# Norms in quarters over two engines, block order in a stage's first slot, and a bank-wise last slot: a two-block transformer on one core

## What is computed

```python
for l in range(2):                                   # first block
    h = rms_norm(x, norm_mix[l])
    x = x + (swa_sb_mixer if l == 0 else hgrn2_mixer)(h, ...)
    x = x + memory_cross_attention(rms_norm(x, norm_cross[l]), rms_norm(mem, norm_mem[l]), ...)
    x = x + conv_ffn(rms_norm(x, norm_ffn[l]), ...)   # up 1024 -> 2 x 2816, conv of 3, silu gate, down
x = layer_norm(ALPHA * x + pool_mixer(x), ...)        # second block; means over 2, 4, 8, 16 tokens
x = layer_norm(ALPHA * x + swiglu(x, ...), ...)
x = layer_norm(ALPHA * x + nsa_mixer(x, ...), ...)
x = layer_norm(ALPHA * x + moe_ffn(x, ...), ...)      # 8 experts, top 2, 2 x 3584 wide
```

## Time and profile before

| | |
|---|---|
| median of 3 runs | 2549.62 us (2549.35 to 2552.17) |
| the profiled execution | 2545.54 us, of it the span of the core 2543.6 us |
| TensorE matmul busy | 2435.7 us, 96% of the span |
| VectorE busy | 1924.6 us, 76% |
| ScalarE busy | 1310.6 us, 52% |
| mean granted TensorE clock | 0.988 of full speed |

### The profile page before, as it was taken

How to read it: one execution, slowest core, us unless ns; L and a number is a source line. 1 busy time by engine, 2 the same in 40 slices (tenths; PEclk the granted TensorE clock), 3 DMA queues, 4 the chain that set the end, 5 groups by cost and what they waited for, 6 DMA issues and landing times.

```text
span 2543.6 us, 43969 instructions
## 1 busy us (share of the span) xinstructions
PE 2435.7 (96%) x18390; PEld 2319.4 (91%) x18390; DVE 1924.6 (76%) x2365; ACT 1310.6 (52%) x1436; POOL 2.4 (0%) x8
## 2 busy tenths in 40 slices
PE   7899999999999999799998889999999999999998
PEld 6689999999999999799897789999999999999996
DVE  6656596888675868754656678888888888888887
ACT  3445333344443333133225357766676767676764
POOL 0000000000000000000000000000000000000000
PEclk9999999999999999999999999999999999999999
DMA  5224245532343455354331159998999999899895
GB/s 215 77 102 148 106 183 179 188 133 100 125 149 116 166 183 183 127 183 180 135 117 59 67 200 364 342 339 333 343 342 340 342 339 343 340 342 341 343 339 211
DMA packets 77283, 557.27 MB, mean 219 GB/s; under 512 B 8609, under 2 KB 8737, under 8 KB 10145
## 3 DMA queue, kind: packets, MB, share of 16 engines
q1 hardware_dynamic: 75888, 547.45, 57.9%
q10 hardware_dynamic: 1008, 6.49, 0.7%
q0 software_dynamic: 192, 0.52, 0.1%
HBM read 552.86 MB, written 1.05 MB: 218 GB/s over the span
## 4 chain that ended last, share of the span: by engine, by line
PE 69%; DVE 4%; ACT 2%; issue 1%; DMA 1%; DVEq 0%; ACTq 0%; SPq 0%
PE ps L1380 12%; PE ps L1382 12%; PE ps L1381 12%; PE ps L837 8%; PE ps L839 8%; PE ps L838 8%; PE ps L929 2%; PE ps L1420 1%; PE ps L900 1%; PE ps L1374 1%; ACT whi L496 1%; DMA raw<-stream 1%; PE ps L1177 1%; PE ps L844 0%; DVE x L1613 0%
## 5 line engine op out<-in xcount | busy, mean ns | idle before, releaser
L1506 DVE TENSOR_TENSOR wlo<-raw,whi 128x2048 fp32r<-128x2048 f32 x519 | 1186.1, 2290 | 318.1 <-ACT whi L496 259.4
L496 ACT ACTIVATE whi<-raw 128x2048 fp32r<-128x2048 f32 x519 | 993.6, 1915 | 580.1 <-PE ps L839 424.6
L837 PE MATMUL ps<-hh,whi 128*128 128x256 f32 x2080 | 599.1, 288 | 26.5 <-DVE hl L1574 21.2
L838 PE MATMUL ps<-hl,whi 128*128 128x256 f32 x2080 | 593.0, 285 | 0.0
L839 PE MATMUL ps<-hh,wlo 128*128 128x256 f32 x2080 | 592.9, 285 | 0.0
L1380 PE MATMUL ps<-whi,hh 128*128 128x256 f32 x1792 | 523.4, 292 | 3.6 <-DVE work L2193 3.6
L1382 PE MATMUL ps<-wlo,hh 128*128 128x256 f32 x1792 | 507.7, 283 | 0.0
L1381 PE MATMUL ps<-whi,hl 128*128 128x256 f32 x1792 | 507.4, 283 | 0.0
L837 PEld LDWEIGHTS ps<-hh,whi 128*128 128x128 f32 x2080 | 403.9, 194 | 31.3 <-DVE hl L1574 24.7
L838 PEld LDWEIGHTS ps<-hl,whi 128*128 128x128 f32 x2080 | 404.1, 194 | 0.3
L839 PEld LDWEIGHTS ps<-hh,wlo 128*128 128x128 f32 x2080 | 403.7, 194 | 0.0
(11 more groups left out here) (329 smaller groups left out, 2782.0 us busy)
## 6 DMA issues: line engine op xcount, KB each, us to landing
raw<-stream SPq DMA_DIRECT2D x519, 1024.0 KB, 4.9
work<-w_in ACTq DMA_DIRECT2D x1, 2240.0 KB, 8.5
stage<-stage_consts ACTq DMA_DIRECT2D x4, 512.0 KB, 4.7
work<-mem_in ACTq DMA_DIRECT2D x2, 1024.0 KB, 4.8
x<-x_in SPq DMA_DIRECT2D x1, 1024.0 KB, 4.8
out<-x SPq DMA_DIRECT2D x4, 256.0 KB, 2.3
const<-consts SPq DMA_DIRECT2D x1, 548.5 KB, 5.9
work<-work POOLq DMA_DIRECT2D x4, 128.0 KB, 2.3
```

The source lines that it names most:

```text
L496: nc.scalar.activation(whi[hi_at(g, odd)][:, :], raw[g % RAWS][:, :], ACT.Copy).then_inc(hi_ready, 1)
L837: mm(out_ap, hi_w, hi_x, start=start, stop=False, **kw)
L838: mm(out_ap, hi_w, lo_x, start=False, stop=False, **kw)
L1506: V.tensor_tensor(wlo[g % RAWS][:, :], raw[g % RAWS][:, :], whi[hi_at(g, odd)][:, :].bitcast(F32), ALU.subtract).then_inc(lo_ready[g % RAW ...
```

## The change

- RMS norms (`rms_norm`, `rms_act`): VectorE scales a quarter; ScalarE rounds it into hh; VectorE makes hl of the quarter before.
- Layer norms (`layer_norm`, `layer_norm_act`): VectorE centres, scales and makes hl; ScalarE squares, shifts (Identity with a bias) and rounds. In the last two norms nothing is rounded.
- The squares of x ahead of the norm of hg_in move from VectorE to ScalarE.
- First slots with waits: both output rows of an input block are done before the next block.
- The last down slot of the three dense layers (`down_last`) goes output by output; each finished bank releases its add on VectorE (`acc_ready`, three times, and `slot_used`); the closing zero matmuls are gone.
- Pool mixer: the first doubling reads x itself, ScalarE fills in its first column; the division by the full window is part of the subtraction, and only the first 16 columns get their own factor (`shorter`); rounding and alpha go to ScalarE.
- Dummy matmuls ahead of first slots: ab_in 14 to 10, ffn0, ffn1 and hg_in 22 to 18, ffn2 and nsa_in 32 to 22; within layer norms 24, 14, 20, 20 to 12 each; ten after ffn0 are gone.

```diff
--- before.py
+++ after.py
...
@@ -361,6 +367,14 @@
...
+        HI_AT = {0: 0, 2: 1, 3: 2, 4: 3, 6: 4, 7: 5, "pool": 6, "ln0": 7, "ln1": 8}
+
+        POOL_PAD = 16
+
+        def pool_sums(i):
+
+            return Wc(4352 * i, NB * (POOL_PAD + BLK)).rearrange("p (b t) -> p b t", b=NB)
...
@@ -512,6 +526,34 @@
...
+            def round_quarter(c, src):
+
+                nc.scalar.activation(hh[:, c * 512:(c + 1) * 512], src[:, c * 512:(c + 1) * 512], ACT.Copy).then_inc(hi_done, 1)
+
+            def rms_act(n):
+
+                norm_act(n, D, 1e-6)
+                for c in range(QUARTERS):
+                    act.wait_ge(norm_scaled, QUARTERS * HI_AT[n] + c + 1)
+                    round_quarter(c, hf)
+
+            def layer_norm_act(i):
+
+                last = i >= 2
+                for c in range(QUARTERS):
+                    act.wait_ge(ln_centred, QUARTERS * i + c + 1)
+                    nc.scalar.activation(hf[:, c * 512:(c + 1) * 512], x[:, c * 512:(c + 1) * 512], ACT.Square).then_inc(squares_ready, 1)
+                norm_act(8 + i, D, 1e-5)
+                for c in range(QUARTERS + 1):
+                    if c < QUARTERS:
+                        act.wait_ge(norm_scaled, QUARTERS * (6 + i) + c + 1)
+                        for b in (2 * c, 2 * c + 1):
+                            ins = nc.scalar.activation(xb(b), xb(b), ACT.Identity, bias=R("ln_b", 8 * i + b))
+                        ins.then_inc(x_ready, 1)
+                    if c and not last:
+                        act.wait_ge(x_ready, QUARTERS * i + c)
+                        round_quarter(c - 1, x)
...
@@ -665,11 +707,14 @@
...
-            norm_act(4, D, 1e-6)
+            for c in range(QUARTERS):
+                act.wait_ge(acc_drained, c + 1)
+                nc.scalar.activation(hf[:, c * 512:(c + 1) * 512], x[:, c * 512:(c + 1) * 512], ACT.Square).then_inc(squares_ready, 1)
+            rms_act(4)
...
@@ -733,15 +778,23 @@
...
+            for g in range(QUARTERS):
+                act.wait_ge(acc_drained, QUARTERS + g + 1)
+                nc.scalar.activation(pool_sums(1)[:, 2 * g:2 * g + 2, POOL_PAD:POOL_PAD + 1], xb(2 * g, 2).rearrange("p (b t) -> p b t", b=2)[:, :, 0:1],
+                                     ACT.Copy).then_inc(pool_first, 1)
+            for g in range(QUARTERS):
+                act.wait_ge(pool_mixed, g + 1)
+                round_quarter(g, hf)
+                nc.scalar.activation(x[:, g * 512:(g + 1) * 512], x[:, g * 512:(g + 1) * 512], ACT.Copy, scale=ALPHA).then_inc(pool_scaled, 1)
...
-            norm_act(8, D, 1e-5)
+            layer_norm_act(0)
...
@@ -854,13 +907,15 @@
...
-                for b in range(2):
-                    for c in range(NB):
-                        if h is not None and s == first and b == 0 and c % 2 == 0:
-                            pe.wait_ge(h_ready, QUARTERS * (h - 1) + c // 2 + 1)
-                        w = slice((b * NB + c) * P, (b * NB + c + 1) * P)
-                        x_hi, x_lo = (t[:, c * BLK:(c + 1) * BLK] for t in (hh, hl)) if src is None else src(c)
-                        last = split_mm(ps[:, bank, b * BLK:(b + 1) * BLK], hi[:, w], lo[:, w], x_hi, x_lo, c == 0, c == NB - 1)
+                waits = h is not None and s == first
+                by_rows = [(b, c) for b in range(2) for c in range(NB)]
+                for b, c in sorted(by_rows, key=lambda bc: bc[1]) if waits else by_rows:
+                    if waits and b == 0 and c % 2 == 0:
+                        pe.wait_ge(h_ready, QUARTERS * (h - 1) + c // 2 + 1)
+                    w = slice((b * NB + c) * P, (b * NB + c + 1) * P)
+                    x_hi, x_lo = (t[:, c * BLK:(c + 1) * BLK] for t in (hh, hl)) if src is None else src(c)
+                    last = split_mm(ps[:, bank, b * BLK:(b + 1) * BLK], hi[:, w], lo[:, w], x_hi, x_lo,
+                                    c == 0 and not (waits and b), c == NB - 1, skip_group_check=waits)
...
@@ -884,6 +939,21 @@
...
+            def down_last(ph, s, a0):
+
+                g = ph.g + s
+                hi, lo = whi[hi_at(g)], wlo[g % RAWS]
+                wait_lo(pe, g)
+                pe.wait_ge(act_ready, a0 + 2 * s + 2)
+                for b in range(NB):
+                    for c in range(2):
+                        m = slice((2 * s + c) * BLK, (2 * s + c + 1) * BLK)
+                        w = slice((c * NB + b) * P, (c * NB + b + 1) * P)
+                        last = split_mm(ps[:, 3 + b // 2, (b % 2) * BLK:(b % 2 + 1) * BLK], hi[:, w], lo[:, w], ahi[:, m], alo[:, m],
+                                        False, c == 1, skip_group_check=True)
+                    if b % 2:
+                        last.then_inc(acc_ready if b < NB - 1 else slot_used, 1)
...
@@ -922,8 +992,10 @@
...
-                            down_slot(ph, s, a0)
-                acc_zero(False, True).then_inc(acc_ready, 1)
+                            if i == 3 and s == ph.n - 1:
+                                down_last(ph, s, a0)
+                            else:
+                                down_slot(ph, s, a0)
...
-            ffn_pe(0, 6, norm=3, idle=22)
-            keep_warm(7, 10)
+            ffn_pe(0, 6, norm=3, idle=18)
...
+            layer_norm_pe(0, lambda c: pe.wait_ge(pool_added, c + 1) if c < 3 else pe.wait_ge(banks_drained, ph.e + 1), 12)
+            ffn_pe(2, 14, norm=8, idle=22)
+            layer_norm_pe(1, lambda c: pe.wait_ge(acc_drained, QUARTERS * 2 + c + 1), 12)
...
@@ -1577,56 +1648,44 @@
...
+            def low_quarter(c, src):
+
+                to_lo(src)(c)
+
+            def rms_norm(n, src, gain, at):
+
+                dve.wait_ge(rstd_ready, n + 1)
+                for c in range(QUARTERS + 1):
+                    if c < QUARTERS:
+                        for b in (2 * c, 2 * c + 1):
+                            ins = V.scalar_tensor_tensor(out=hf[:, b * BLK:(b + 1) * BLK], in0=src[:, b * BLK:(b + 1) * BLK],
+                                                         scalar=R(gain, at + b), in1=rstd[:, :], op0=ALU.mult, op1=ALU.mult)
+                        ins.then_inc(norm_scaled, 1)
+                    if c:
+                        dve.wait_ge(hi_done, QUARTERS * HI_AT[n] + c)
+                        low_quarter(c - 1, hf)
+
+            def layer_norm(i, g_at, last=False):
...
-
-                dve.wait_ge(rstd_ready, n + 1)
-                staged(scaled(src, gain, at), to_hi(hf), to_lo(hf))
...
-                def centre(c):
-                    for b in (2 * c, 2 * c + 1):
-                        step(V.scalar_tensor_tensor(out=xb(b), in0=ps[:, MEAN_BANK[i], 0:BLK], scalar=-1.0 / D, in1=xb(b),
-                                                    op0=ALU.mult, op1=ALU.add))
-
-                staged(centre, lambda c: squares(x, c))
+                        ins = V.scalar_tensor_tensor(out=xb(b), in0=ps[:, MEAN_BANK[i], 0:BLK], scalar=-1.0 / D, in1=xb(b),
+                                                     op0=ALU.mult, op1=ALU.add)
+                    ins.then_inc(ln_centred, 1)
                 dve.wait_ge(rstd_ready, 9 + i)
-
-                def scale(c):
-                    for b in (2 * c, 2 * c + 1):
-                        step(V.scalar_tensor_tensor(out=xb(b), in0=xb(b), scalar=R("ln_g", g_at + b), in1=rstd[:, :],
-                                                    op0=ALU.mult, op1=ALU.mult))
-
-                def shift(c):
-                    for b in (2 * c, 2 * c + 1):
-                        ins = V.tensor_scalar(xb(b), xb(b), R("ln_b", g_at + b), None, ALU.add)
-                    ins.then_inc(x_ready, 1)
-
-                def hi_of(c):
-                    dve.wait_ge(x_ready, QUARTERS * i + c + 1)
-                    to_hi(x)(c)
-
+                for c in range(QUARTERS + 2):
+                    if c < QUARTERS:
+                        for b in (2 * c, 2 * c + 1):
+                            ins = V.scalar_tensor_tensor(out=xb(b), in0=xb(b), scalar=R("ln_g", g_at + b), in1=rstd[:, :],
+                                                         op0=ALU.mult, op1=ALU.mult)
+                        ins.then_inc(norm_scaled, 1)
+                    if c >= 2 and not last:
+                        dve.wait_ge(hi_done, QUARTERS * HI_AT[f"ln{i}"] + c - 1)
+                        low_quarter(c - 2, x)
...
-                    staged(scale, shift)
                     dve.wait_ge(x_ready, QUARTERS * (i + 1))
-                else:
-                    staged(scale, shift, hi_of, to_lo(x))
 
...
@@ -1722,14 +1781,13 @@
...
-                dve.wait_ge(acc_ready, layer + 1)
-                for c in range(QUARTERS + 1):
-                    if c < QUARTERS:
-                        V.scalar_tensor_tensor(out=xs(c), in0=xs(c), scalar=alpha, in1=ps[:, 3 + c, :], op0=ALU.mult,
-                                               op1=ALU.add).then_inc(acc_drained, 1)
-                    if layer == 0 and c:
-                        dve.wait_ge(acc_drained, c)
```

(37 more changed lines are left out.)

55 lines of the change are left out of this document (24 added, 31 removed).

## The result

The changed kernel took 2509.93 us, median of 4 runs (2503.41 to 2514.20), beside 2550.89 us (2549.35 to 2555.09) for the kernel before on the same chip: a ratio of 0.9848, 95% interval 0.9828 to 0.9869. Forecast were 2514.7 us and a range of 2508 to 2524. The profiled execution took 2510.95 us with a span of 2509.0 us (2508.7 forecast), beside 2543.6 before.

The account below looks back on a forecast made before the run. The dense part was taken as TensorE-bound, 48 matmuls a slot, leaving seams where TensorE waits on a norm. Nine terms summed to 34.9 us, taken from the timed median 2549.62: 2514.7 us, range 2508 to 2524.

Parts of the forecast that it names:

- The RMS norms: First slots of ffn0 and ffn1: start 2.38 us after the norm's root (r) instead of 4.83, 5.0 us gained together.
- ab_in: First stage, TensorE cold: last issue at 34.0 instead of 35.4, 1.4 us gained; 2.6 or 0.5 depending on the clock.
- Into hg_in: Layer 0's last slot into hg_in: 4.2 us gained, 3 to 5, with half a chance of a 1.7 us clock drop.
- Into the pool mixer: Layer 1's end into the pool mixer: TensorE starts 7.0 us earlier, 6.8 us gained, 5.5 to 7.5.
- The bound of 0.7 us: Pool mixer's slot: 0 to 0.7 us longer at half clock, as TensorE is as cold as before.
- Layer norms: Four norms: root (r) 1.4 us sooner; first slots of ffn2 and nsa_in at r + 3.9, 3.0 gained at each.
- Norm 2's 1.4: Norm ahead of the router and experts: 1.4 us gained, with 24 dummy matmuls pacing the router behind its root.
- The sum of the sites: Nine terms over all edited seams add up to 34.9 us gained.
- rival 2: The clock takes part of the gain: drops at five of ten seams cost 8 us, giving 2523; chance 0.16.
- Rival 3: The gain goes on into a later wait, in hg_in's slots or the weights' first loads: 2522; chance 0.06.
- Rival 4: ScalarE's moved work queues behind weight roundings at every seam; only block order and last slots gain: 10 us, 2540; chance 0.02.
- Rival 5: Slower: ScalarE switches tables at shifts and copies, 46 us of loads against 35 gained, some 2560; chance 0.02.

Follow-up runs that it names:

- experiment 1: Changed kernel with first slots that have waits going row by row again instead of block by block; 2522.53 us, ratio to before 0.9903.
- experiment 3: Changed kernel with the rounding of the RMS norms back on VectorE; 2522.57 us, ratio to before 0.9890.
- experiment 2: Changed kernel with the last down slot of the three dense layers closed by zero matmuls again, then the four adds; 2516.17 us, ratio to before 0.9868.
- experiment 4: Changed kernel with squares, shift and rounding of the four layer norms back on VectorE; 2521.78 us, ratio to before 0.9891.
- experiment 5: Changed kernel with ScalarE's four squares ahead of hg_in placed before its last weight rounding of layer 0; 2505.26 us, ratio to before 0.9835.
- first trace: The profiled execution of the changed kernel, unedited; 2510.95 us, span 2509.0 us.
- second trace: The changed kernel once more, unedited, traced and timed on another chip; median 2511.14 us, ratio to before 0.9857.
- experiment 9: Changed kernel with the pool mixer's VectorE part as before, the bank-wise last slot kept; 2517.43 us, ratio to before 0.9869.
- experiment 7: Changed kernel with 54 instead of 20 dummy matmuls ahead of the pool mixer's slot; 2506.24 us, ratio to before 0.9834.
- experiment 6: Changed kernel with 20 dummy matmuls added between layer 0's last slot and the sums ahead of hg_in; 2507.82 us, ratio to before 0.9841.
- experiment 8: Changed kernel with the layer norms' shift on VectorE, squares and rounding still on ScalarE; 2518.12 us, ratio to before 0.9881.
- experiment 10: Changed kernel with 10 instead of 24 dummy matmuls ahead of the router; 2508.73 us, ratio to before 0.9839.
- experiment 11: Changed kernel with the edits of experiment 5, experiment 7 and experiment 10 together; 2501.50 us, ratio to before 0.9814.

## Why the prediction was right, point by point

**The RMS norms.** r + 2.38 was forecast for the slot and r + 2.44 came; the copy out of SBUF that no row of before showed, taken as 0.62 between 0.42 and 0.62, took 0.63. Two readings of the earlier trace rows were a little off. r was 304.28 and not 304.36 before, so VectorE's first instruction came 0.11 behind it and not 0.03; this is in both kernels and cancels. And before, the slot did not go on from 309.91 without a stop: there was one more at 310.85, which cost 0.2 us with what followed it. So ffn0 gave 2.7 instead of 2.5. What order and sharing are worth is shown by experiments 1 and 3. ffn1 gave 4.0: the prediction took its rows before to be those of ffn0, but the last matmul of that slot came at r + 12.1 and not r + 10.9. This 1.3 is a half clock in the kernel before's slot that the changed one's trace doesn't have, and no merit of the edit (experiments 1, 2 and 4 show nothing there but their own edit).

**ab_in.** The start at r + 2.36 is the mechanism's. The 1.6 is not shown to be the edit's: with the same instructions the last matmul of this slot came between r + 8.4 and r + 10.8 in the traces of kernels that don't edit it, as the clock rose sooner or later, and at r + 10.8 in the kernel before.

**Into hg_in.** The mechanism (squares behind the weight rounding, sums 2.6 us late) is shown by experiment 5. The term was 4.2 with half a chance of a drop; in the first trace the drop came (3.5), in the second it didn't (5.0).

**Into the pool mixer.** 7.2 us gained at its start, 7.0 forecast, of which 2.5 are the last slot's (experiment 2) and 4.7 the mixer's (experiment 9). The bound of 0.7 us lost to the half clock was too low: it was 1.0 in the first trace, and 0.2 in the second. Experiment 7 shows that the idle time causes it.

**Layer norms.** r 1.4 sooner at all four, the slot at r + 4.0, the output at r + 4.2: shown by experiment 4, which takes back 1.40 four times. Norm 2's 1.4 arrived at r (1.40) but only 0.6 at the experts. This is the one term of which less than half came, and not by the chance of one execution: in all ten traces with the changed kernel's norm 2 and 24 dummies ahead of the router (both of the changed kernel, experiments 1 to 3 and 5 to 9, of which 8 differs in the shift alone) the experts start 30.5 to 31.1 us behind the root, with a mean granted clock of 0.57 to 0.59 over r + 12 to r + 20. In the kernel before and in experiment 4 they start 29.7 to 29.8 behind it, with 0.79. With 10 dummies (experiments 10 and 11) they start 28.6 to 28.7 behind, also with 0.79. Why the shorter norm is followed by more of the half clock stays open.

**The sum and the median.** The sum of the sites was right to 0.2 us and the span to 0.3, both in part by luck. In the sum, ffn1's 1.3 from the clock made up for hg_in, the pool mixer and norm 2, which gave 2.1 less than forecast; in the span the unedited stretches, -2.1 to +1.4, nearly cancelled. In the second trace the sites give about 37 us (5.0 at hg_in, 7.0 at the pool mixer, 1.1 at ab_in). The step that was off is the last: I carried the 4.1 us between the profiled execution of before and its median over to the changed kernel. That difference was no property of the kernel; the profiled execution of before was a favourable one (5.3 us below the later median), the one after was 1.0 above its own. The medians differ by 41.0 us on the first chip and 37.8 on the last, against the 34.9 of the sum, and that remainder of 3 to 6 us is of the size of the clock's scatter; which stretches hold it isn't settled. The measured 2509.93 lies 4.8 below the forecast and 1.9 above the low end of the range.

**The rivals.** In the first trace the clock (rival 2) took 1.5 us at hg_in, 1.0 at the pool mixer and 0.8 ahead of the experts, and gave 1.3 back at ffn1: right in kind, 2 us net instead of 8. Rival 3 falls by experiments 1 and 5: seams add. Rival 4 was true at one seam alone, the one named. Rival 5: no table load stands at a shift, a square or a rounding; L552, L546 and L532 have none in the whole trace, and it has 44 loads like the one before. (The sum for this rival counted three layer norms where four shift; with four it is 8 x 1.283, some 10 us, more.) That agrees with the Trainium skill, "ScalarE: Activation LUTs", Table sets, on copy and identity.

## What to carry to other kernels

Cost a seam from the end of the value that all wait for (here r), engine by engine and quarter by quarter, and split a chain over two engines even where the single instruction is dearer on the second: what counts is the longer chain. When work moves to another engine, look at what stands ahead of it in that engine's queue, as an instruction that waits for the slot just ending holds back everything behind it. Compare two kernels slot by slot at the same event, not by totals: here differences of 1.4 us repeat to 0.05 us in the traces, while medians scatter by 4.
